# A two-layer decoder trunk on one core: five of the second layer's low weight parts made by GpSimd instead of VectorE

## The reference, cut to what matters

```python
h = jnp.einsum('btd,de->bte', x, w_in)          # 1024 -> 9776, split into 16 parts
y_a = pool_mixer(...) * silu(pz)
y_b = cb * short_conv(cc * cx, ...) * silu(cz)
y_c = nsa_mixer(q, kc, vc, ks, vs, kw, vw, ...) * silu(az)     # compressed, selected, window attention
merged = g_a * (y_a @ proj_a) + g_b * (y_b @ proj_b) + g_c * (y_c @ proj_c)
out = layer_norm(ALPHA * x + merged @ w_out)
```

## Time and profile before

| what | value |
|---|---|
| median of 3 runs | 802.36 us (801.02 to 804.2) |
| the profiled execution | 804.0 us |
| its span | 802.3 us |
| PE busy | 770.2 us, 96% of the span |
| DVE busy | 557.0 us, 69% |
| ACT busy | 400.2 us, 50% |
| POOL busy | 90.5 us, 11% |
| low parts on DVE | 202 of 1.231 us each, 248.3 us in all |

### The profile page before, as it was taken

The page is one execution under the profiler, slowest core; times in us unless marked ns, Lnnn a source line. Parts: engine busy times, 40 slices in busy tenths (PEclk is TensorE's granted clock), DMA queues, the critical chain, the costliest instruction groups (busy, mean ns, idle before and its releaser), DMA issues.

```text
span 802.3 us, 16955 instructions
## 1 busy us (share of the span) xinstructions
PE 770.2 (96%) x6354; PEld 720.4 (90%) x6354; DVE 557.0 (69%) x1038; ACT 400.2 (50%) x793; POOL 90.5 (11%) x166
## 2 busy tenths in 40 slices
PE   8999979999999999999999978799999999999995
PEld 8998778888889999999879978788988999999994
DVE  4564679997679575657465666799886876665664
ACT  5442456666555444443345442676755464444423
POOL 2333430000133100000000034200000000000000
PEclk9999999999999999999999998999999999999998
DMA  8988756533868766555348786636348356665521
GB/s 313 285 272 294 228 179 216 190 103 107 293 227 261 233 179 181 179 181 175 106 136 229 257 246 209 235 113 211 103 123 308 118 183 184 184 183 175 181 93 55
DMA packets 42331, 154.95 MB, mean 193 GB/s; under 512 B 6416, under 2 KB 7440, under 8 KB 41616
## 3 DMA queue, kind: packets, MB, share of 16 engines
q1 hardware_dynamic: 33952, 115.55, 45.8%
q0 software_dynamic: 8304, 38.37, 14.4%
HBM read 145.77 MB, written 13.34 MB: 198 GB/s over the span
## 4 chain that ended last, share of the span: by engine, by line
PE 87%; DVE 6%; DMA 2%; ACT 2%; issue 1%; SPq 0%; DVEq 0%; ACTq 0%
PE bank L664 22%; PE bank L665 22%; PE bank L666 22%; PE bank L682 3%; PE bank L882 3%; DMA ring<-weights_dram 2%; DVE w_lo L1199 2%; PE bank L826 1%; PE bank L832 1%; PE bank L837 1%; PE bank L675 1%; PE bank L1003 1%; PE bank L923 1%; PE bank L1012 1%; PE bank L862 1%
## 5 line engine op out<-in xcount | busy, mean ns | idle before, releaser
L1199 DVE TENSOR_TENSOR w_lo<-ring,w_hi 128x1024 fp32r<-128x1024 f32 x202 | 248.3, 1231 | 155.7 <-ACT w_hi L1021 151.8
L664 PE MATMUL bank<-x_hi,w_hi 128*128 128x264 f32 x1208 | 352.5, 292 | 2.2 <-DVE w_lo L1199 2.2
L666 PE MATMUL bank<-x_lo,w_hi 128*128 128x264 f32 x1208 | 344.5, 285 | 0.0
L665 PE MATMUL bank<-x_hi,w_lo 128*128 128x264 f32 x1208 | 344.4, 285 | 0.0
L1021 ACT ACTIVATE w_hi<-ring 128x1024 fp32r<-128x1024 f32 x202 | 213.3, 1057 | 68.9 <-PE bank L666 34.0
L664 PEld LDWEIGHTS bank<-x_hi,w_hi 128*128 128x128 f32 x1208 | 229.9, 190 | 6.6 <-issue 3.3
L665 PEld LDWEIGHTS bank<-x_hi,w_lo 128*128 128x128 f32 x1208 | 229.9, 190 | 0.4
L666 PEld LDWEIGHTS bank<-x_lo,w_hi 128*128 128x128 f32 x1208 | 228.8, 189 | 0.0
L664 PE MATMUL bank<-h_rounded,w_hi 128*128 128x264 f32 x352 | 102.2, 290 | 0.0
L665 PE MATMUL bank<-h_rounded,w_lo 128*128 128x264 f32 x352 | 100.2, 285 | 0.0
L1073 ACT ACTIVATE h<-bank 128x264 f32<-128x264 f32 x88 | 34.6, 393 | 99.0 <-PE bank L666 90.6
(11 more groups left out here) (253 smaller groups left out, 994.6 us busy)
## 6 DMA issues: line engine op xcount, KB each, us to landing
ring<-weights_dram SPq DMA_DIRECT2D x208, 512.0 KB, 3.7
cache_a<-kcmp_dram POOLq DMA_DIRECT2D x32, 128.0 KB, 3.8
cache_b<-vcmp_dram POOLq DMA_DIRECT2D x32, 128.0 KB, 3.5
cache_a<-ksel_dram POOLq DMA_DIRECT2D x32, 128.0 KB, 4.2
cache_b<-vsel_dram POOLq DMA_DIRECT2D x32, 128.0 KB, 2.6
cache_a<-kwin_dram POOLq DMA_DIRECT2D x2, 2048.0 KB, 11.7
cache_b<-vwin_dram POOLq DMA_DIRECT2D x2, 2048.0 KB, 8.9
kv_dram<-h POOLq DMA_DIRECT2D x2, 1584.0 KB, 6.9
```

The costliest lines, as they stand in the source:

```text
L664: pe.matmul(out, w_high[:, k0 + k, :], high, start=(k == 0), stop=False)
L665: pe.matmul(out, w_rest[:, k0 + k, :], high, start=False, stop=False)
L666: ins = pe.matmul(out, w_high[:, k0 + k, :], rest, start=False, stop=(k == kn - 1))
L1199: dve.tensor_tensor(w_lo[:, slot % RING], ring[:, slot % RING], w_hi[:, d % HI_RING].bitcast(F32), ALU.subtract).then_inc(w_lo_ready, 1)
```

## The change

In the second layer the low parts of dense tiles 8, 10, 12, 14 and 16 (the ninth to the seventeenth, every second one) are computed by POOL with the same subtraction. DVE leaves them out. PE waits for those five on a semaphore of POOL's, for the others on DVE's with the count lowered by those left out. On POOL the five stand ahead of everything else of the second layer, so ahead of the store of keys and values; each waits for its own high part.

```diff
+POOL_SPLITS = [SPLIT_NO[SLOT_OF[1, "dense", n]] for n in range(8, 18, 2)]
...
+                for d in POOL_SPLITS if l else []:
+                    slot = SPLIT_SLOTS[d]
+                    pool.wait_ge(w_hi_ready, d + 1)
+                    go()
+                    pool.tensor_tensor(w_lo[:, slot % RING], ring[:, slot % RING], w_hi[:, d % HI_RING].bitcast(F32),
+                                       ALU.subtract).then_inc(w_lo_ready_by_pool, 1)
+
                 pool.wait_ge(roped, l * len(ROPED) + 4)
...
                     d = SPLIT_NO[i]
-                    pe.wait_ge(w_lo_ready, d + 1)
+                    if d in POOL_SPLITS:
+                        pe.wait_ge(w_lo_ready_by_pool, POOL_SPLITS.index(d) + 1)
+                    else:
+                        pe.wait_ge(w_lo_ready, d + 1 - sum(1 for n in POOL_SPLITS if n < d))
...
                     for n, d in enumerate(SPLIT_AT.get((l, step, i), [])):
-                        if which is not None and n != which:
+                        if which is not None and n != which or d in POOL_SPLITS:
                             continue
```

More of the change, by code:

```diff
@@ L398, in trunk @@
         w_hi_ready, w_lo_ready = sem("w_hi_ready"), sem("w_lo_ready")
+        w_lo_ready_by_pool = sem("w_lo_ready_by_pool")
         output_ready = sem("output_ready")
```

## The result

The changed kernel takes **808.28 us** (median of 6 runs, 807.61 to 810.91); the kernel before took 803.74 us (median of 6, 801.02 to 804.28) beside it. The ratio is 1.0071, 95% interval [1.0054, 1.0089]. A later comparison on another occasion gave 807.41 against 802.95: 1.0057 [1.0038, 1.0076]. The ratios aren't the quotients of the two medians, which are 1.0057 and 1.0055: the medians differ by 4.5 us both times, the ratios stand for 4.6 and 5.7 us: the change costs 4.5 to 5.7 us. The forecast was slower, 810.0 in a range of 804.0 to 815.5; time and sign lie in it. Its parts do not: 5.7 of its 7.6 us stood for something that never happened, and what did happen is two to three times as large as the 1.9 us of its only other term.

What follows compares the result with a forecast made beforehand. PE was taken as the bound (87% of the chain that ended last), DVE's load costing it some 0.1 us in the stretch. 4.0 + 1.7 + 1.9 = 7.6 us on the median of 802.36 gave 810.0 us, range 804.0 to 815.5.

Steps and rivals of the forecast that it cites:

- Step 1: Ahead of dense tile 8, second layer: 6.05 us before POOL's low part starts make PE 4.0 us late.
- rival (b): At tile 8: no delay of the low part and no clock loss, the rest as forecast; chance 0.18.
- (c): Ahead of tile 8: the delay of POOL's low part is more than 6.05 us; range's upper end 815.5; chance 0.16.
- (d): At tiles 8 and 13: no delay ahead of w8, and POOL's subtraction takes under 1.65 us; chance 0.05.
- Step 2: Behind the 4.0 us gap at tile 8: PE's granted clock falls, +1.7 us.
- Step 3: At tile 13: w14 on POOL starts first, w13 on DVE waits for it, PE starts late, +1.9 us.
- D: Length of one low part (1024 elements) on POOL, taken as 2.0 us.
- Rival (e): DVE's swap copies are shut out too, by w12 and w14: about 1.6 us more, 811.6; chance 0.03.
- Step 4: Behind tile 13: w16 and the store leaving some 11 us later cost nothing, up to 0.5 us for the range.

Runs made afterwards that it cites:

- both repairs: Against the changed kernel, store ahead of w16, plus tile 14 on DVE (four tiles): 803.78 us, 1.0003; or w14 behind w13 (five tiles): 804.13 us, 1.0013.

## Why the prediction was right, and where it wasn't

- **Step 1, the start of w8 (+4.0 forecast, 0 measured): wrong.** The 6.05 us in this step is the author's price for the ISA at L571, taken for a transfer of code: the middle between the 3.8 us of a page load and the 8.3 us of the constants from issue to use, 13.26 to 21.55. No run shows such a term in the changed kernel; the runs show about 0.1 us in its place, w8 starting 0.27 us behind its high part, as rival (b) held. (Of the rivals in the chances, (b) is the forecast without steps 1 and 2, (c) puts more than 6.05 us into step 1, and (d) has no step 1 and a subtraction on POOL of under 1.65 us.) Only with the broadcast ahead of it did w8 start 6.95 us late, in one profile. That this is a transfer, of code or of anything else, was an assumption that no trace bears out.
- **Step 2, the clock (+1.7 forecast): wrong with it.** Its 0.58 is the granted clock of 506 to 510, behind a gap of 3.30 us in PE's weight loads. There was no wait at tile 8, and no fall: the granted clock is 1.00 in every window of 4 us from 424 to 448 of the first profile. But the fall itself came at another place: behind the 2.95 us at tile 13 in one of two profiles, for 1.4 us. The forecast had tied the clock to step 1 and forgot it at step 3.
- **Step 3, the collision at tile 13 (+1.9 forecast, 2.8 measured): the mechanism was right, two sizes were off.** w14 starts at 446.25, as forecast to the hundredth, and is ahead of w13. D was 2.40 instead of 2.0, 0.40 us. The step had w13 itself asked for and held, with 1.09 us left after POOL's end; in fact DVE was still at its copies and a copy was held, so that after POOL's end (448.65) came the rest of the copy, one more copy and a whole w13, up to 450.28: 1.63 us, 0.54 more. 1.9 + 0.4 + 0.5 = 2.8. Rival (e), given 0.03, had this: swap copies are shut out, by w12 and by w14. It priced w12's group, which was through in time (its last copy started at 440.33, POOL at 440.45), and not w14's.
- **Step 4, the late store (nothing forecast, 0.5 in the range): most likely too low.** The changed kernel stands 0.44% (1.0057 against 1.0013, all five tiles) to 0.68% (1.0071 against 1.0003) above those with both repairs, collision and store together. The seven pairs that differ in the store alone are 0.04 to 0.41% apart, 0.3 to 3.3 us, the middle one 0.18% (1.4 us). Only the two with nothing on POOL were measured side by side, and both of their intervals hold 1. The step let the loads land within 3.3 to 7.3 us, and the one of 460.24 took no more, 7.41. Where it failed is what it made of that: the 7.3 was itself the load behind the store, a kind of load that takes 6.4 to 7.6 us wherever the store goes, and the step left out SP's issues, which take 2.5 us longer for four and hold up the load behind them.
- **The sum.** 7.6 us were forecast, 4.5 to 5.7 measured. The eight pairs that differ in the collision alone (tile 14 on DVE, or w14 behind w13) are 0.13 to 0.50% apart, the middle of them 0.3%, about 2.4 us; the profiles have 2.2 at tile 13 (2.8 less the 0.6 of w12), and more where the clock falls. The forecast came near by luck: two errors went against each other, a wait at tile 8 that wasn't there and a loss at tile 13 and behind it that was too small. The base helped too: the forecast stood on 802.36, and the kernel before had a median of 803.74 in the six runs beside the changed one, so that a cost 3 us too large ended only 1.7 us off in the time. Had steps 1 and 2 been dropped, the forecast would have been 802.36 + 1.9 = 804.3, with no difference that can be measured, and wrong by 4 us.

**Still open.** Whether, and why, the store costs more with low parts on POOL: 0.36% and 0.41% between kernels with four low parts on POOL that differ in the store, but 0.04 to 0.19% with five, against 0.07 to 0.14% without any. (All those with low parts on POOL are from separate comparisons.) The profiles' second column shows the direction, but only some 1 us of the 3 us. The intervals with and without the late store don't touch in the pairs with four ([1.0021, 1.0058] and [1.0025, 1.0062] against [0.9987, 1.0019]), but that the cost is larger than that of the store alone is within the scatter; a longer series of runs, and more than one profile of each, would be needed. It wasn't tried to give the store another queue.

## What to carry to other kernels

Before an operation moves to POOL, list for each one what DVE asks for in the 2 or 3 us behind its start: one short copy caught there (0.28 us became 2.47 here) holds up everything behind it, and the price (here 2.80 us at tile 13) is POOL's whole operation plus the rest of DVE's list up to the tile that PE wants, not only an operation that has two inputs. Put POOL's operation behind the low part that is due first, and leave a transfer that POOL issues ahead of work that has time; the second is the smaller gain here, and the less certain. An instruction that only the built program has is not yet a cost: the one here took 0.1 us, and w8 started 6.95 us late only when a broadcast had run on POOL before it. And when a row has a longest value, such as the 7.3 us of a weight load, ask what stood beside it before taking it for a bound.

## What was not expected of the hardware

- POOL's subtraction of 128x1024 shuts out one-input DVE copies of 64x128: 2.47 and 2.37 us instead of 0.28. It seems to work both ways: w10 on POOL took 2.79 instead of 2.40, having started at 434.66 while DVE's last rope operation ran (2.49 to 2.80 in seven other profiles):

```profile
434.48 0.71 DVE L1295 TENSOR_TENSOR h<-h,z 128x528 f32<-128x528 f32 x1
```

- A broadcast on POOL made the next subtraction there start 6.95 us late (one profile), 161 us after it; without the broadcast the same subtraction started 0.27 us behind its high part.
- A store of 1584 KB in flight slows SP's issues: four issues of 16.5 KB each that take 2.65 us otherwise took 3.5 to 5.5 in all eight profiles with the late store just ahead of them, with low parts on POOL or without, and 4.4 in that of both repairs with five tiles, where they stand 1.2 us behind the early store and cost nothing.
- Behind PE waits of 2.93 to 2.95 us at tile 13 the granted clock stayed at 1.00 in two profiles (the changed kernel, and the one with the store ahead of w16) and fell in two: in the second of the changed kernel, for 1.4 us, and in that with the broadcast, where it was 0.50 in 460 to 464 and the loss at tile 13 5.3 us instead of 2.8. A cost of this kind is one of chance and belongs in the range.
